# Expert layers: the key stage in whole slabs with a smaller search, the value stage on scaled weights with 16-bit low products

## The chip, the cores and the metric

One core of a Trainium2 chip runs the whole program. The metric is the device time in microseconds (us) from start to end of one execution; the median of several is compared.

## The reference

Two transformer layers on 256 tokens of width 2048, in f32: a state-space mixer, then sliding-window attention with a memory part, each followed by an output projection, a layer norm, an expert layer (PEER) and another layer norm. Only the expert layer matters here. For each token and each of 8 heads it scores 2 x 128 keys, takes the 16 best of each half, the 16 best of their 256 sums, and a softmax over those; the 128 chosen experts of 16384 then work as follows.

```python
sc = jnp.einsum('bshtd,htkd->bshtk', q, subkeys)
top_s, top_i = lax.top_k(sc, PEER_TOPK)
cand = top_s[..., 0, :, None] + top_s[..., 1, None, :]
best_s, best_c = lax.top_k(cand.reshape(b, s, PEER_HEADS, PEER_TOPK * PEER_TOPK), PEER_TOPK)
...
gate = jax.nn.softmax(best_s, axis=-1)
hid = jnp.einsum('td,tkd->tk', xb, u[ib])
act = jax.nn.gelu(hid, approximate=False) * gb
out = jnp.einsum('tk,tkd->td', act, v[ib])
x = layer_norm(DEEPNORM_ALPHA * x + out, g, b)
```

## The kernel before

Weights of 1 MiB slabs stream through the chip. SyncE loads a slab (2048 f32 columns in each of 128 partitions, two pieces) into one of three buffers `raw`. ScalarE copies each piece into `wh` (function `hi`, line 597), rounded to the fast matmul format fp32r; VectorE subtracts that from the original and so has the low rest (`lo`, lines 1743 and 1746). TensorE multiplies by the high and the low part (helper `mm`, line 1043), so that the sum is nearly f32. `wh` and the low buffers have four pieces. A semaphore `piece_used` counts pieces that TensorE is done with, `hi_ready` and `lo_ready` those made; a raw buffer is loaded anew when VectorE has lowered all of it.

The expert layer handles 64 of the tokens by rows and 192 densely:
- The 64 tokens: GpSimd gathers for each of 64 pairs of experts two rows to 128 partitions (1 MiB, two buffers). VectorE takes the product of a gathered key row with the token (a dot, L1928) and later adds the gathered value row, weighted, to an accumulator (L2126).
- The 192 tokens: key stage, 128 slabs of 128 experts each: h = gelu(U x) for all experts; then every h is multiplied by a gate, zero where the expert isn't chosen; value stage, 128 slabs: sum of V h.

Key stage, per slab (`slab_u`): for each of two pieces 8 products with `wh` over 384 columns (x's high and low part), then 8 with the 16-bit low part over 192. The low weights are scaled up by 2^16 so that 16 bits hold them (`scaled_up`). A fold (`cross` by ScalarE, L637, then one product) adds the side column group, and ScalarE applies gelu (L777). The first 64 slabs' h stay in SBUF (`KEPT`), the others' go to HBM and back.

During the first 64 key slabs VectorE makes the search, in 16 units of one head and 128 tokens: maxima, their places, removal, sums, maxima again; what it does beside the search is written out by hand in `UNIT_FILL`, L for a low of one piece, D for a dot. Some 18 dots stand there and 46 in the last 64 slabs (`DOT_PIECE`). Chosen places become expert numbers by one-hot comparison with `iota` and a sum, per unit. TensorE replicates the numbers (`replicate`) before slab 20 (`REP_TRIP`), and GpSimd can gather from then on. In the last 64 key slabs the gates are spread out: 48 groups of four tokens, each a comparison on VectorE (`compare`, L2051), scaled copies on ScalarE (`gate_rows`, L792) and 8 products on TensorE (`spread`).

Value stage, per slab (`slab_v`): for each of 2 pieces and 2 halves of 512 columns, five products: the first 64 of the 192 tokens (here "split": their high and low part side by side as one operand of 128 columns) with the high and the low weights, the other 128 ("whole") high by high, high by low, low by high. 20 products of 512 columns, all fp32r, on unscaled weights. ScalarE makes the activations' high part (L856) and its double (L857), VectorE the low part (L1760), and the gated h for the later slabs (L2105). The last two slabs have their own order (`last_slabs_v`), and a layer norm follows.

## Time and profile before

| | us |
|---|---|
| median of three executions | 3279.53 (3274.16 to 3283.69) |
| the profiled execution, its own time | 3274.78 |
| its span, first to last instruction | 3273.0 |
| TensorE / VectorE / ScalarE / GpSimd busy | 3196.3 / 2773.5 / 1997.0 / 406.6 |
| moved by DMA | 969.07 MB, mean 296 GB/s |
| TensorE's granted clock, mean | 0.996 of full |

Times in the trace are microseconds from the span's start, durations of groups are means in nanoseconds. An engine's busy time is the union of its instructions' times; matmuls are pipelined, so one's duration is longer than the distance to the next one's start. "L1043" is line 1043 of the kernel.

### The profile page before, as it was taken

What the parts mean: (1) busy time and instruction counts of PE and PEld (TensorE: products, weight loads), DVE (VectorE), ACT (ScalarE), POOL (GpSimd) and SP (SyncE); (2) the same over time, 40 slices, a digit from 0 to 9 for tenths busy, and PEclk for the clock granted to TensorE, in tenths of its full rate; (3) what the DMA queues carried; (4) which work ended last, traced back from release to release, by engine and by line L of the source; (5) the groups of instructions that cost most, each with busy time, mean ns of one, the idle gap of its engine ahead of it and who ended that gap; (6) DMA issues with size and microseconds to landing.
All of it is one profiled execution on the core that took longest, in us unless ns stands there. A gap on an engine that the chain in (4) does not pass through costs nothing. (4 is left out here: it accounts for less than half of the span.)

```text
span 3273.0 us, 52190 instructions
## 1 busy us (share of the span) xinstructions
PE 3196.3 (98%) x19468; PEld 2762.0 (84%) x19468; DVE 2773.5 (85%) x4026; ACT 1997.0 (61%) x3631; POOL 406.6 (12%) x266
## 2 busy tenths in 40 slices
PE   9999999999999999999999999999999999999998
PEld 8888888889888888888888887888888888888887
DVE  5775669999999888888887756999999988888887
ACT  4444556556898755555555545655688875555555
POOL 0000000011111122222100000001111112222220
PEclk9999999999999999999999999999999999999999
DMA  7553345698999989999984344578899999999995
GB/s 273 183 183 140 116 161 192 257 342 339 379 379 378 373 335 372 362 371 367 365 305 156 117 152 158 197 278 338 335 390 380 373 369 366 368 370 368 363 368 224
DMA packets 169221, 969.07 MB, mean 296 GB/s; under 512 B 18912, under 2 KB 52704, under 8 KB 55648
## 3 DMA queue, kind: packets, MB, share of 16 engines
q1 hardware_dynamic: 132192, 698.61, 56.2%
q0 software_dynamic: 36864, 268.45, 22.3%
q8 instruction: 80, 1.31, 0.1%
q14 instruction: 85, 0.70, 0.1%
HBM read 951.26 MB, written 15.73 MB: 295 GB/s over the span
## 5 line engine op out<-in xcount | busy, mean ns | idle before, releaser
L597 ACT ACTIVATE wh<-raw 128x1024 fp32r<-128x1024 f32 x1264 | 1335.5, 1060 | 833.5 <-PE ps L1043 663.9
L1043 PE MATMUL ps<-xx,wh 128*128 128x384 f32 (+1 forms) x5504 | 1333.7, 358 | 6.8 <-DVE xx L1755 4.0
L1043 PE MATMUL ps<-wh,act 128*128 128x512 f32 x3584 | 1190.6, 390 | 0.4 <-issue 0.2
L1746 DVE TENSOR_TENSOR wl<-raw,wh 128x1024 fp32r<-128x1024 f32 x752 | 905.9, 1221 | 323.8 <-ACT wh L597 322.2
L1043 PEld LDWEIGHTS ps<-xx,wh 128*128 128x128 f32 x5504 | 955.5, 189 | 73.5 <-issue 5.7
L1043 PE MATMUL ps<-wl,act 128*128 128x512 f32 x2304 | 897.6, 390 | 0.0
L1043 PEld LDWEIGHTS ps<-wh,act 128*128 128x128 f32 x3584 | 673.8, 188 | 142.0 <-DVE wl L1746 1.0
L1743 DVE SCALAR_TENSOR_TENSOR halves<-raw,wh 128x1024 f16<-128x1024 f32 x512 | 615.2, 1213 | 63.5 <-ACT wh L597 63.1
L1043 PEld LDWEIGHTS ps<-wl,act 128*128 128x128 f32 x2304 | 433.2, 188 | 89.7
L1043 PE MATMUL ps<-halves 128*128 128x192 f16 x4096 | 428.3, 248 | 22.5 <-DVE halves L1743 20.6
L1043 PEld LDWEIGHTS ps<-halves 128*128 128x128 f16 x4096 | 312.7, 98 | 112.4 <-issue 62.8
L1043 PE MATMUL ps<-xx,wl 128*128 128x256 f32 x1408 | 393.9, 280 | 0.0
L1711 POOL DMA_INDIRECT arena<-in_urows,idx x128 | 150.9, 1179 | 1907.3 <-DVE idx L2018 1072.0
L1711 POOL DMA_INDIRECT arena<-in_v,idx x128 | 246.8, 1928 | 839.4 <-DVE arena L2126 818.4
L2126 DVE SCALAR_TENSOR_TENSOR arena<-arena,hid 128x2048 f32<-128x2048 f32 x128 | 300.2, 2345 | 2.2 <-DMA arena<-in_v,idx 2.1
L1928 DVE SCALAR_TENSOR_TENSOR arena<-arena 128x2048 f32<-128x2048 f32 x128 | 292.0, 2281 | 0.0
L1043 PEld LDWEIGHTS ps<-xx,wl 128*128 128x128 f32 x1408 | 266.2, 189 | 0.5
L792 ACT ACTIVATE hot_w<-hot,x_space 128x128 f16<-128x128 f16 x768 | 242.1, 410 | 8.0 <-DVE hot L2051 8.0
L637 ACT ACTIVATE cross<-ps 128x192 fp32r<-128x192 f32 (+1 forms) x272 | 89.8, 330 | 124.5 <-PE ps L1043 122.2
L1043 PE MATMUL ps<-cross,ident_r 128*128 128x192 f32 (+1 forms) x272 | 92.0, 338 | 16.9 <-ACT cross L637 15.7
L777 ACT ACTIVATE arena<-ps 128x192 f32<-128x192 f32 x128 | 42.1, 329 | 108.3 <-PE ps L1043 108.2
L1043 PE MATMUL ps<-arena 64*128 64x128 f32 (+9 forms) x712 | 93.3, 317 | 7.5 <-DVE arena L2004 4.6
(225 smaller groups left out, 1751.2 us busy)
## 6 DMA issues: line engine op xcount, KB each, us to landing
raw<-in_u SPq DMA_DIRECT2D x256, 1024.0 KB, 7.1
raw<-in_v SPq DMA_DIRECT2D x256, 1024.0 KB, 7.4
raw<-in_w SPq DMA_DIRECT2D x118, 1024.0 KB, 4.8
h_scratch<-hring SPq DMA_DIRECT2D x128, 96.0 KB, 7.3
hring<-h_scratch SPq DMA_DIRECT2D x128, 96.0 KB, 7.1
arena<-in_memT SPq DMA_DIRECT2D x4, 512.0 KB, 7.2
raw<-in_w SPq DMA_DIRECT2D x4, 512.0 KB, 7.8
arena<-in_xT SPq DMA_DIRECT2D x4, 512.0 KB, 8.5
```

Source lines behind the costliest of these rows:

```text
L597: nc.scalar.activation(wh[:, j, :], raw_piece(p), ACT.Copy, scale=W_UP if scaled_up(p) else 1.0)\
L637: nc.scalar.activation(cross[:, 0:n], ps[:, bank, n:2 * n], ACT.Copy).then_inc(cross_out, 1)
L777: nc.scalar.activation(h_kept[:, k, :] if kept else hring[:, j, :], ps[:, j, 0:ND], ACT.Gelu, scale=W_DOWN).then_inc(evac_done, 1)
L792: nc.scalar.activation(hot_w[:, q % 2, w, t, :], one_hot(q, 0, t), ACT.Copy, scale=gate_hl[w][:, of // NS, of % NS:of % NS + 1]).then_inc( ...
L1043: return nc.tensor.matmul(out, lhs, rhs, start=start, stop=stop, **kw)
L1711: pool.indirect_dma_start(out=gbuf[n % SLOTS], out_offset=None, in_=rows_of, in_offset=bass.IndirectOffsetOnAxis(ap=idx[:, j:j + 1], axis=0))\
L1743: v.scalar_tensor_tensor(out=wl16[:, j, :], in0=raw_piece(p), scalar=W_UP, in1=wh[:, j, :].bitcast(F32), op0=ALU.mult, op1=ALU.subtract).t ...
L1746: v.tensor_tensor(wl[:, j, :], raw_piece(p), wh[:, j, :].bitcast(F32), ALU.subtract).then_inc(lo_ready, 1)
L1928: v.scalar_tensor_tensor(out=rows_u, in0=rows_u, scalar=1.0, in1=xrep, op0=ALU.mult, op1=ALU.mult, accum_out=hid[:, j:j + 1]).then_inc(slo ...
L2126: v.scalar_tensor_tensor(out=vacc, in0=rows_v, scalar=hid[:, j:j + 1], in1=vacc, op0=ALU.mult, op1=ALU.add).then_inc(slot_free, 1)
```

## The change

What it does:
- Key stage: high copies and lows are made for a whole slab by one instruction (`hi_slab`, `low_slab`), TensorE multiplies all 16 high parts, then all 16 low ones; the fold stands after the tenth high product. `piece_used` now counts the high and the low part of a slab.
- Search: two units at a time, interleaved; 112 candidate sums instead of 256 (4 x 16 and 12 x 4); the copy of the scores is gone; the one-hot selection is made for four units together in 16-bit numbers (`batch`). 24 dots in the first 64 slabs, 40 in the last. Replication before slab 16, the gates' transposition and setup at slabs 48 and 51 instead of 64 and after.
- Gates: one comparison for both halves of a group.
- Value stage: its weights are scaled by 2^16 too; what is added to its sums (the residual through `ident_up`, the accumulator, the gathered rows' weights, the norm's epsilon) is scaled likewise. The low products are 16-bit: four over 512 columns for the whole tokens and, for the split ones, only high weights' rest by a 16-bit copy of the activation (`a16`, a fourth copy on ScalarE), 64 columns wide, two products side by side on the two halves of the array. The 12 high products stay.

The diff, cut to its core:

```diff
-REP_TRIP = 5
+REP_TRIP, SEL_TRIP = 4, 12
...
-UNIT_FILL = ([("L", "", "L", "", "L", "L", "")] * 2 + [("L", "L", "L", "", "L", "L", "")]
-             + [("L", "L", "L", "L", "L", "L", "")] * 7 + [("LL", "LL", "LL", "LL", "LDL", "LL", "DL")]
-             + [("LDLL", "", "LDLL", "L", "LDLL", "L", "L")] * 4 + [("LDLL", "", "LLL", "L", "LDLL", "L", "L")])
-UNIT_TAIL = ("L", "LD", "L", "L", "L", "", "")
-SPARED = (2, 5)
...
+PAIR_FILL = ([("L", "", "L", "", "L", "", "L", "")] * 2 + [("L", "L", "L", "L", "", "", "", "")]
+             + [("S", "S", "", "S", "S", "", "S", "S"), ("S",) * 8,
+                ("S", "S", "", "S", "SD", "S", "D", "S"), ("S", "S", "SD", "S", "S", "SD", "S", ""),
+                ("S", "SD", "", "S", "S", "D", "S", "S")])
+LAST_FILL = ("S", "D", "S", "", "SD", "", "S", "", "S")
+REST_FILL = ("S", "SD", "SD", "SD", "S", "SD", "SD", "S", "SD", "SD") * 2
+BATCH = 4
+KEY_PAIRS = 4 * TOPK + (TOPK - 4) * 4
+EXP_SLAB, SETUP_SLAB = 40, 51
+DOT_SLABS = (1, 2, 4, 6, 7)
...
-    return P_U0 <= p < P_V0 or P_U1 <= p < P_V1
+    return P_U0 <= p < P_INB or P_U1 <= p < P_END
...
+        def hi_slab(p):
+
+            act.wait_ge(piece_used, p - (RING - 1))
+            act.wait_ge(lo_ready, p - 2)
+            n, j = p // 2, p % RING
+            act.wait_ge(raw_full[n % RAW_SLABS], 16 * (n // RAW_SLABS + 1))
+            nc.scalar.activation(wh[:, j:j + 2, :], raw[:, n % RAW_SLABS, :].rearrange("p (e c) -> p e c", e=2), ACT.Copy,
+                                 scale=W_UP if scaled_up(p) else 1.0).then_inc(hi_ready, 2)
...
+            def v_slab(k):
+                p, s = v0 + 2 * k, k % 2
+                act.wait_ge(piece_used, p - (RING - 1))
+                if k < KEPT:
+                    source = h_kept[:, k, :]
+                else:
+                    act.wait_ge(act_ready, layer * (S_EXP - KEPT) + k - KEPT + 1)
+                    source = act_t[:, s, :]
+                nc.scalar.activation(ffn_h[:, s, :], source, ACT.Copy).then_inc(acth_ready, 1)
+                nc.scalar.activation(ffn_dup[:, s, :], source[:, 0:NS], ACT.Copy).then_inc(dup_ready, 1)
+                if k:
+                    hi_slab(p)
+                act.wait_ge(piece_used, max(p - 2, v0))
+                nc.scalar.activation(a16[:, s, :], source, ACT.Copy).then_inc(a16_ready, 1)
...
+            pe.wait_ge(hi_ready, piece + 2)
+            for kc in range(KC):
+                last = mm(both, part(wh, kc), xx[:, kc, :, NS:], kc == 0, False, skip_group_check=True)
+                if kc == FOLD_AT and side_of is not None:
                     fold(side_of, 1 - par_, side_t0)
-                if then is not None:
-                    then(e)
+            last.then_inc(piece_used, 1)
+            if then is not None:
+                then(0)
+            pe.wait_ge(lo_ready, piece + 2)
+            for kc in range(KC):
+                if x_from is not None and kc % XS == 0:
+                    pe.wait_ge(x16_ready, x_from + kc // XS + 1)
+                last = mm(side, part(wl16, kc), x16[:, kc // XS, kc % XS, :], False, kc == KC - 1, skip_group_check=True)
+            last.then_inc(piece_used, 1)
...
+        def v_high(s, e, q):
+            w_hi = wh[:, 2 * s + e, q * 512:(q + 1) * 512]
+            return w_hi, ps[:, 2 * e + q, :], ps[:, 4 + 2 * e + q, :]
+
+        def split_low(s, e):
+
+            w = wl16[:, 2 * s + e, :]
+            mm(ps[0:NS, 2 * e, :], a16[:, s, 0:NS], w[:, 0:512], False, False, skip_group_check=True)
+            return mm(ps[NS:P, 2 * e + 1, :], a16[:, s, 0:NS], w[:, 512:PC], False, False, skip_group_check=True)
+
+        def whole_low(s, e, q):
+            return mm(ps[:, 4 + 2 * e + q, :], a16[:, s, NS:ND], wl16[:, 2 * s + e, q * 512:(q + 1) * 512], False, False,
+                      skip_group_check=True)
 
         def slab_v(piece, chunk, dup, s, opens=False):
 
             pe.wait_ge(actl_ready, chunk + 1)
             pe.wait_ge(dup_ready, dup)
             both, a_h, a_l = act[:, s, 0:2 * NS], ffn_h[:, s, NS:ND], ffn_l[:, s, NS:ND]
-            for e in range(2):
-                j = 2 * s + e
-                pe.wait_ge(lo_ready, piece + (e + 1))
-                for q in range(2):
-                    w_hi, w_lo = (w[:, j, q * 512:(q + 1) * 512] for w in (wh, wl))
-                    split, whole = ps[:, 2 * e + q, :], ps[:, 4 + 2 * e + q, :]
-                    mm(split, both, w_hi, opens, False, skip_group_check=True)
-                    mm(split, both, w_lo, False, False, skip_group_check=True)
-                    mm(whole, a_h, w_hi, False, False, skip_group_check=True)
-                    mm(whole, a_h, w_lo, False, False, skip_group_check=True)
-                    last = mm(whole, a_l, w_hi, False, False, skip_group_check=True)
-                last.then_inc(piece_used, 1)
-
...
+            def low_slab():
...
+                v.scalar_tensor_tensor(out=wl16[:, j:j + 2, :],
+                                       in0=raw[:, p // 2 % RAW_SLABS, :].rearrange("p (e c) -> p e c", e=2), scalar=W_UP,
+                                       in1=wh[:, j:j + 2, :].bitcast(F32), op0=ALU.mult, op1=ALU.subtract)\
+                    .then_inc(lo_ready, 2)
...
+                    own.mark(v.tensor_tensor(sums[:, 0:4 * TOPK].rearrange("p (a b) -> p a b", a=4),
+                                             tv[:, 0, 0:4].unsqueeze(2).broadcast_to([P, 4, TOPK]),
+                                             tv[:, 1, :].unsqueeze(1).broadcast_to([P, 4, TOPK]), ALU.add))
+                    own.mark(v.tensor_tensor(sums[:, 4 * TOPK:].rearrange("p (a b) -> p a b", b=4),
+                                             tv[:, 0, 4:TOPK].unsqueeze(2).broadcast_to([P, TOPK - 4, 4]),
+                                             tv[:, 1, 0:4].unsqueeze(1).broadcast_to([P, TOPK - 4, 4]), ALU.add))
...
+                elif step == 6:
+                    own.mark(v.tensor_tensor(pick.rearrange("p w k a u -> p (w k) a u"),
+                                             rank.rearrange("p w k u -> p (w k) u").unsqueeze(2)
+                                             .broadcast_to([P, 2 * TOPK, TOPK, BATCH]),
+                                             iota_u.unsqueeze(1).broadcast_to([P, 2 * TOPK, TOPK, BATCH]), ALU.is_equal))
+                elif step == 7:
+                    flat = pick.rearrange("p w k a u -> p w k (a u)")
+                    own.mark(v.tensor_tensor(flat, flat, top_f[:, b % 2].rearrange("p w a u -> p w (a u)").unsqueeze(2)
+                                             .broadcast_to([P, 2, TOPK, TOPK * BATCH]), ALU.mult))
+                else:
+                    for w in range(2):
+                        own.mark(v.tensor_reduce(
+                            sel[:, w, b * BATCH * TOPK:(b + 1) * BATCH * TOPK].rearrange("p (u k) -> p k u", u=BATCH),
+                            pick[:, w].rearrange("p k a u -> p k u a"), AX.X, ALU.add))
...
-                quad = slice(4 * q, 4 * q + 4)
-                for w in range(2):
-                    v.tensor_tensor(hot[:, q % 2, w, :].rearrange("p (a j t) -> p a j t", a=4, t=4),
-                                    iota_h.rearrange("p a (j t) -> p a j t", t=4),
-                                    sel_t[:, w, quad].unsqueeze(1).unsqueeze(1).broadcast_to([P, 4, P // 4, 4]),
-                                    ALU.is_equal).then_inc(onehot_ready, 1)
+                v.tensor_tensor(hot[:, q % 2, :, :].rearrange("p w (j t) -> p w j t", t=4),
+                                iota_h.rearrange("p (j t) -> p j t", t=4).unsqueeze(1).broadcast_to([P, 2, P, 4]),
+                                sel_t[:, :, 4 * q:4 * q + 4].unsqueeze(2).broadcast_to([P, 2, P, 4]),
+                                ALU.is_equal).then_inc(onehot_ready, 2)
...
+            def gated(k):
+
+                n = layer * (S_EXP - KEPT) + k - KEPT
+                dve.wait_ge(h_loaded[k % BODY], 16 * (n // BODY + 1))
+                dve.wait_ge(actl_ready, c0 + k - 1)
+                dve.wait_ge(a16_ready, layer * S_EXP + k - 1)
+                v.tensor_tensor(act_t[:, k % 2, :], hring[:, k % BODY, :], gate_of[:, k - KEPT, :],
+                                ALU.mult).then_inc(act_ready, 1)
```

## Rows read from the trace of the kernel before

**Rows 1.** Page, part 1: busy us, share of the span, instructions, each engine

```profile
PE 3196.3 (98%) x19468; PEld 2762.0 (84%) x19468; DVE 2773.5 (85%) x4026; ACT 1997.0 (61%) x3631; POOL 406.6 (12%) x266
```

**Rows 2.** Windows, layer 0: length, busy us of each engine, clock, DMA share, GB/s

```profile
520.32:814.14 293.82, 281.63 (x2156) 257.77 (x2155) 282.49 (x629) 167.89 (x262) 31.93 (x20) 0.99 0.79 295
814.14:1132.84 318.70, 307.43 (x2495) 279.36 (x2493) 295.94 (x362) 281.98 (x687) 48.04 (x47) 1.00 0.97 379
1133.94:1712.86 578.92, 578.81 (x2569) 479.37 (x2570) 497.82 (x515) 321.30 (x510) 122.54 (x62) 0.99 0.93 353
603.00:613.00 10.00, 7.69 (x48) 6.62 (x46) 9.96 (x30) 3.09 (x5) 0.00 (x0) 0.83 0.63 209
1000.00:1050.00 50.00, 48.40 (x397) 44.19 (x396) 46.46 (x58) 44.56 (x109) 7.31 (x7) 1.00 1.00 393
1200.00:1250.00 50.00, 50.00 (x223) 41.38 (x222) 44.12 (x41) 27.77 (x44) 15.66 (x7) 1.00 0.96 374
1550.00:1600.00 50.00, 50.00 (x222) 41.39 (x221) 43.21 (x50) 27.91 (x45) 9.41 (x5) 1.00 0.95 361
```

**Rows 3.** Timeline, TensorE in the key stage: start us, us, what

```profile
556.09 1.64 PE L1043 MATMUL ps<-xx,wh 128*128 128x384 f32 x8
557.57 0.83 PE L1043 MATMUL ps<-halves 128*128 128x192 f16 x8
...
558.36 1.58 PE L1043 MATMUL ps<-xx,wh 128*128 128x384 f32 x8
559.78 0.83 PE L1043 MATMUL ps<-halves 128*128 128x192 f16 x8
560.39 0.42 PE L1043 MATMUL ps<-xx,wh 128*128 128x384 f32 x1
```

**Rows 4.** Timeline, TensorE at half-wide products

```profile
530.10 0.83 PE L1043 MATMUL ps<-halves 128*128 128x192 f16 x8
530.87 3.71 PE L1043 MATMUL ps<-ident_r,arena 128*64 128x128 f32 x64
534.51 0.44 PE L1043 MATMUL ps<-xx,wh 128*128 128x384 f32 x1
```

**Rows 5.** Timeline, TensorE where the expert indices are replicated

```profile
605.88 0.83 PE L1043 MATMUL ps<-halves 128*128 128x192 f16 x8
609.00 0.49 PE L1043 MATMUL ps<-arena 128*128 128x128 f32 x2 [2.29 <-DVE arena L2004]
```

**Rows 6.** Timeline, VectorE: one search unit, and a dot with comparisons

```profile
539.03 0.29 DVE L1949 COPY arena<-arena 128x256 f32<-128x256 f32 x1
...
553.07 0.29 DVE L1949 COPY arena<-arena 128x256 f32<-128x256 f32 x1
...
1000.20 1.21 DVE L1743 SCALAR_TENSOR_TENSOR halves<-raw,wh 128x1024 f16<-128x1024 f32 x1
1001.34 2.28 DVE L1928 SCALAR_TENSOR_TENSOR arena<-arena 128x2048 f32<-128x2048 f32 x1
...
1003.55 0.80 DVE L2051 TENSOR_TENSOR hot<-x_space,sel_t 128x512 f16<-128x512 f16 x2
```

**Rows 7.** Groups, VectorE, 530 to 620 us: xcount, busy us, mean ns

```profile
L1989 DVE FIND_INDEX8 arena<-arena 128x8 uint32<-128x128 f32 x14 | 3.8, 284 | 0.0
...
L1951 DVE FIND_INDEX8 arena<-arena 128x8 uint32<-128x256 f32 x6 | 2.5, 419 | 0.0
```

**Rows 8.** Timeline, TensorE beside a gate group

```profile
898.21 0.64 PE L1043 MATMUL ps<-hot_w,hot 128*128 128x128 f16 x8
898.66 0.59 PE L1043 MATMUL ps<-xx,wh 128*128 128x384 f32 x2
```

**Rows 9.** DMA issues, second key half and value stage: KB, median us to landing

```profile
raw<-in_u SPq DMA_DIRECT2D x52, 1024.0 KB, 8.2
...
raw<-in_v SPq DMA_DIRECT2D x108, 1024.0 KB, 7.4
```

**Rows 10.** Groups, ScalarE, value stage: a copy of 2048 elements

```profile
L870 ACT ACTIVATE arena<-arena 64x2048 f32<-64x2048 f32 x1 | 1.9, 1919 | 0.0
```

467 lines of the change are left out of this document (242 added, 225 removed).

## The prediction

> **What bounds the kernel now.** I read the page first, then the windows by stage. TensorE is busy 98% of the span of 3273.0 us [rows 1]. But a busy share of a pipelined engine hides short stalls, so the second view matters more: the expert layer has three stages [rows 2], the key stage's first 64 slabs (294 us), its last 64 with the gate work beside them (319 us) and the 128 value slabs (579 us). Layer 1 repeats them. Together they are some 2380 of 3273 us; outside them only details of two layer norms change.
>
> The reader is to see that each stage has another neighbour at its limit. In the first, VectorE is busy 282.5 of 293.8 us. In the second, the DMA engines are busy 97% of the time. In the value stage TensorE never idles (578.8 of 578.9), with DMA at 93% on average; so only there is a TensorE instruction saved worth its full time, until the next limit.
>
> TensorE's own floor comes from the timeline [rows 3]: eight high products take 1.42 to 1.48 us, eight 16-bit ones 0.62, a fold 0.17; a key slab without any wait takes 560.39 - 556.09 = 4.30 us. A value slab is 20 products in 578.9 / 128 = 4.52 us [rows 2], 0.226 each.
>
> **Key stage, TensorE.** The whole-slab order goes high to low and back once instead of twice. The first group after a low one takes 1.48 instead of 1.42 [rows 3], so 0.06 is saved: floor 4.24 us, 64 x 0.06 = 4 us per half, if the other engines follow. The fold now comes some 0.5 us earlier in the slab and wants ScalarE's copy earlier.
>
> **Key stage, first half (-8 us a layer).** 63 slab intervals at 4.30 and the 64 small products in 534.51 - 530.87 = 3.64 us [rows 4] are 275 us; measured is 294, so 19 us are lost. What loses them:
> - The wait for the expert indices. TensorE stands before the product at 609.00 [rows 5]; it starts 609.00 - 605.88 = 3.12 us after the start of a group that takes 0.62, so 2.5 us, and after that idle stretch the granted clock falls to the lower level (1.2 GHz) for a while: 0.83 on the mean over those 10 us [rows 2], some 1.7 us more. After the change the indices come about slab 13, by the order written out, and are wanted at slab 16. I take -4.5.
> - VectorE. A search unit with six lows takes 553.07 - 539.03 = 14.04 us [rows 6]; less 6 x 1.14 (a low from its start to the next one's start, 1001.34 - 1000.20) that is 7.2 us. Sixteen units: 115 us. New unit: the copy of the scores goes; the 256 candidates become 112; the one-hot selection goes to batches of four units. Durations [rows 7] overlap by some 0.08 us; 128 more elements cost 0.135 us. That gives 3.8 us a unit, 61 us. A batch: two 16-bit operations of 2048 elements, which I price at the rate of the 16-bit comparison (two of 512 elements in 0.80 us [rows 6]: 0.36 each, start to start, 1.2 for 2048; at the f32 rate 2.2), two reductions of 1024 (1.1 each), and seven small ones: 5.8 us, up to 8. Four: 23 to 32. The search falls from 115 to 84 (93).
> - Lows as slabs: one of 2048 takes what the dot takes, 2.21 us start to start, against 2 x 1.14: 0.07 x 62 = 4 us less. Six dots more (24 for 18): +13 us.
>
> Sum on VectorE: -31 + 13 - 4 = -22 us of 294, so it no longer bounds the whole half. Locally it does: in the third pair of units four steps of a batch stand between lows, and slab 2 is then lowered some 2.6 us late; pairs 6 and 7 with their dots ask for about 33 us in the time of seven slabs (30), some 4 us. And 14 dots stand in the last 20 slabs: 1.7 MiB = 1.78 MB a slab, at 385 GB/s 4.63 us instead of 4.24, +7 us over those 20, where 3 are lost today. Sum: -4.5 (indices) - 4 (floor) - 10 (waits between slabs 10 and 44 now) + 2.6 + 4 + (7 - 3) = -8. Bounds: -19 (all waits gone) and +2.
>
> **Key stage, second half (-14 a layer).** Floor 64 x 4.24 + 48 x 0.45 (a gate group, 898.66 - 898.21, [rows 8]) = 293 us. Bytes: 64 slabs, 40 rows instead of 46, and 64 stores of 0.098 MB: 115 MB. The rate to divide by is what a full window shows: share 1.00 at 393 [rows 2]; I take 382 to 390, so 296 to 302, with a little loss 303 us against 318.7: I keep -14, since layer 1 repeats to within 1% only. What TensorE waits for ScalarE stays about as it is: that copies a slab in one instruction (2048 elements in 1.92 us, [rows 10]), but has to be done sooner. Bounds 0 and -24.
>
> **Value stage (-17 a layer).** TensorE: 12 high products of 0.226 = 2.71. The low ones now are 16-bit: 4 of 512 columns at, by [rows 3] (0.62/8 for 192), 0.21 = 0.86, and four half-wide ones in two pairs. That two half-wide products run side by side the trace shows: their 64 records fill 3.64 us [rows 4], 0.057 each, while two records of a full-width product of the same columns and type take 0.49 us with the pipeline's end in it [rows 5], 0.11 each by what is left. So a pair costs one: 0.43 for the four. Changing to half width and back costs something: the last full-width product starts about 530.10 + 7 x 0.083 = 530.68, the half-wide ones at 530.87, 0.19 for 0.083; I take 0.1 each way, 0.2 a slab. Sum 4.20 us, 0.32 less than today, 41 us over 128 slabs. (The Trainium skill, "TensorEngine Tiling (Array Packing)", Key Properties, says that changing the tiling mode drains the engine; it gives no time.)
>
> But DMA takes over. While h is kept in SBUF a slab brings 1.049 MB and 37/62 of a gathered row: 1.674 MB; later 1.049 + 27/56 rows + 0.098 of h = 1.652 MB. At 4.52 us that is 370 and 365 GB/s, and [rows 2] show 374 at a share of 0.96 and 361 at 0.95. Taken to a share of 0.985 that is some 382 and 374, and the slab can't be shorter than 4.38 and 4.42. 118 slabs at 4.40, ten without gathers at 4.20: 561 us, against 579 and, in layer 1, a little less: -17 on the mean. VectorE then needs 2.2 + 0.27 + 0.6 x 2.26 + small = 3.85 of 4.40, ScalarE gets a fourth copy but stands at 321 of 579 us [rows 2]. Bounds: -41, where DMA gives way, and 0.
>
> The Trainium skill puts the HBM limit of one core at about 358 GB/s ("DMA: Bandwidth & Descriptors", Where 436 GB/s comes from) and a core streaming alone at about 425 ("HBM Reference", Specifications). By the first the value stage could gain nothing: 1.674 MB / 358 = 4.68 us, more than today, but [rows 2] already stand above it, so the trace disagrees and it gets no chance. By the second DMA would need 3.94 us and TensorE would bound at 4.20, rival A below; no window of this trace reaches it over 50 us.
>
> Layer norms, the scaling of the accumulator (one ScalarE copy beside idle time), the moved gate setup: nothing, each hidden beside TensorE work; if uncovered, some 2 us each.
>
> **Sum.** 2 x (-8 - 14 - 17) = -78 us. The profiled execution took 3274.78; the median of three is 3279.53, 0.1% above. On the median's footing: about 3201. Changes under 0.3% (10 us) can't be told from none.
>
> **Rivals.**
> - A: TensorE bounds the value stage (DMA reaches over 400 GB/s): 2 x (-41 - 20 - 10) = -142: 3138. For: the value stage's share of 0.96 at 374 is not yet 1.00. Against: where it is 1.00 the rate was 393, and 4.20 us a slab want 399. Chance 0.17.
> - B: the value stage keeps its pace, because DMA is full as it is: only the key stage gains, 2 x -22: 3235. For: at 0.96 the share that is left is small, and a transfer that is late once is not made up. Against: the second key half runs at a share of 0.97 over 319 us [rows 2]. Chance 0.20.
> - C, the slower one: the ring of three raw slabs. A raw slab is free again only when one copy and one low of the whole slab are done, about 1.9 + 2.2 = 4.1 us after landing, while now the last piece is done 3.3 after it. The loop must close in 3 slabs: today 3 x 4.52 = 13.6 us. Landing 7.4 [rows 9] + 4.1 + up to 2.3 behind an accumulation is 13.8; with the 8.2 of the key stage 14.6, 4.87 us a slab: 118 x 0.33 = +39 a layer, less 22 in the key stage: 3279.5 + 34 = 3313. It decides where landing and queueing exceed 9.5 us. Against: the prefetch absorbs single late ones. Chance 0.06.
> - D: the gains are eaten: VectorE falls behind in the search (batches at the f32 rate and more) and DMA holds the value stage: 3280 +- 10. Chance 0.05.
> - My forecast: 0.52, by itself 3172 to 3230.
>
> Range: B with its edge above, A just below: 3135 to 3245 leaves out C, D and half of A, 0.19. Faster by over 0.3%: forecast, A and most of B, 0.87; same 0.06; slower 0.07.
>
> **What would show it.** Value slab interval 4.35 to 4.45 us, DMA share at or above 0.98 there, and ScalarE's copies waiting for DMA instead of for TensorE. First half of the key stage near 286 us, with no clock drop about slab 20; second near 303. Half-wide products starting in pairs, with 0.1 us lost before and after. The sum is wrong if the value slab comes out at 4.2 (A) or stays at 4.5 (B), if landing rises beyond 9 us (C), or if TensorE waits long for 16-bit lows in the first twenty key slabs (D).

## The result, and the profile after

Three more executions and the profiled one of the changed kernel have a median of 3234.29 us (3227.44 to 3248.78); the kernel before, run beside them, 3280.01. The medians differ by 46 us; the ratio, here and below formed from the means, is 0.9868, 95% interval 0.9831 to 0.9905: 1.3% less. Forecast was 3201, with a range of 3135 to 3245: the time lies in the range, near its upper end, but just outside the 3172 to 3230 that was given to the forecast's own mechanism. The profiled execution took 3227.44 us (3274.78 before), its span is 3225.6 (3273.0 before): of the -78 us of the sum it shows -47, so the sum was 31 too large.

The engines over the whole span, against [rows 1]:

```profile
PE 3147.4 (98%) x19468; PEld 2512.1 (78%) x19468; DVE 2667.2 (83%) x3291; ACT 1985.3 (62%) x3383; POOL 567.8 (18%) x266
```

The windows by stage of layer 0, against [rows 2] (same columns); the value stage stands as its first and second half. The fifth line is the stretch in which the indices are replicated now, the sixth the start of the experts in layer 1:

```profile
521.47:811.01 289.54, 277.44 (x2144) 264.72 (x2142) 255.50 (x445) 155.90 (x200) 45.64 (x26) 0.99 0.83 316
811.01:1117.19 306.18, 299.62 (x2497) 285.36 (x2496) 277.12 (x242) 276.21 (x623) 66.27 (x42) 1.00 0.98 379
1118.29:1402.95 284.66, 275.30 (x1281) 166.25 (x1282) 234.53 (x161) 162.99 (x253) 93.95 (x35) 1.00 0.92 357
1407.58:1683.85 276.27, 275.85 (x1260) 165.38 (x1259) 245.81 (x222) 164.48 (x253) 76.54 (x27) 1.00 0.94 367
...
586.00:596.00 10.00, 10.00 (x77) 9.66 (x76) 8.72 (x32) 5.96 (x7) 1.09 (x1) 1.00 0.68 228
...
2040.00:2080.00 40.00, 36.88 (x301) 35.08 (x299) 32.05 (x105) 19.37 (x27) 0.00 (x0) 0.91 0.56 205
```

By stage, both layers, after less before, beside the forecast for a layer:

| us | layer 0 | layer 1 | forecast |
|---|---|---|---|
| key stage, first 64 slabs | -4.3 | +0.6 | -8 |
| key stage, last 64 slabs | -12.5 | -15.4 | -14 |
| value stage | -13.4 | -11.8 | -17 |
| between key and value stage | 0.0 | +0.9 | 0 |
| outside (start, between the layers, end) | +8.4 in all | | 0 |

VectorE went from 282.5 to 255.5 busy us in the first stage (-27; forecast -22), and the first stage still gained next to nothing. The value stage's second half has TensorE busy without a stall; its first half moves fewer bytes a second and stalls.

TensorE in the second half of the value stage (timeline: start, us, instruction, count):

```profile
1509.66 0.38 PE L1069 MATMUL ps<-halves 128*64 128x512 f16 x2
1509.98 3.02 PE L1069 MATMUL ps<-wh,act 128*128 128x512 f32 x12
1512.84 1.59 PE L1069 MATMUL ps<-halves 128*128 128x512 f16 x8
1514.36 3.02 PE L1069 MATMUL ps<-wh,act 128*128 128x512 f32 x12
1517.22 1.59 PE L1069 MATMUL ps<-halves 128*128 128x512 f16 x8
```

High products 1512.84 - 1509.98 = 2.86 us, low ones 1514.36 - 1512.84 = 1.52: a slab takes 4.38, again and again. The forecast counted 2.71 + 1.49 = 4.20 for TensorE and 4.38 to 4.42 for DMA. The interval came out as forecast (4.35 to 4.45), but here TensorE sets it.

TensorE in the first key half, against [rows 3] to [rows 5]; the bracket is idle time and what ended it:

```profile
523.91 1.26 PE L1069 MATMUL ps<-xx,wh 128*128 128x384 f32 x6
528.29 1.49 PE L1069 MATMUL ps<-halves 128*128 128x192 f16 x16 [3.12 <-DVE halves L1967]
...
589.25 0.41 PE L1069 MATMUL ps<-arena 128*128 128x128 f32 x2
...
591.36 1.26 PE L1069 MATMUL ps<-xx,wh 128*128 128x384 f32 x6
592.46 1.49 PE L1069 MATMUL ps<-halves 128*128 128x192 f16 x16
593.73 1.99 PE L1069 MATMUL ps<-xx,wh 128*128 128x384 f32 x10
595.56 0.25 PE L1069 MATMUL ps<-cross,ident_r 128*128 128x192 f32 x1
595.65 0.54 PE L1069 MATMUL ps<-xx,wh 128*128 128x384 f32 x2
...
751.72 1.52 PE L1069 MATMUL ps<-halves 128*128 128x192 f16 x11 [2.37 <-DVE halves L1967]
```

Three things are to be seen. The wait for the indices and the clock drop behind it are gone (589.25 has no bracket; clock 1.00 from 586 to 596, 0.83 in [rows 2]). Slab 2 waits 3.12 us for its low part (forecast 2.6). A key slab is 1.10 + 1.27 + 1.83 + 0.09 = 4.29 us, not 4.24: against 4.30 in [rows 3] the whole-slab order is worth 0.01, not 0.06.

VectorE just before the last of these waits:

```profile
740.59 2.28 DVE L1967 SCALAR_TENSOR_TENSOR halves<-raw,wh 128x2048 f16<-128x2048 f32 x1
746.17 2.29 DVE L1985 SCALAR_TENSOR_TENSOR arena<-arena 128x2048 f32<-128x2048 f32 x1 [3.30 <-DMA arena<-in_urows,idx]
...
749.38 2.28 DVE L1967 SCALAR_TENSOR_TENSOR halves<-raw,wh 128x2048 f16<-128x2048 f32 x1
```

It stood 3.30 us before rows that had not landed, with the low part that TensorE wanted behind them in its order.

### The profile page after: what moved, and what is told of

It reads as the page before. It is cut to its first block, busy times and chain, and to the rows that moved or that the text cites. A ratio compares the mean times of both kernels' runs of the same rounds, so it can differ in the third digit from the quotient of the medians.

```text
span 3225.6 us, 51808 instructions
## 1 busy us (share of the span) xinstructions
PE 3147.4 (98%) x19468; PEld 2512.1 (78%) x19468; DVE 2667.2 (83%) x3291; ACT 1985.3 (62%) x3383; POOL 567.8 (18%) x266
## 4 chain that ended last, share of the span: by engine, by line
PE 41%; DMA 15%; DVE 9%; ACT 6%; issue 3%; ACTq 0%; SPq 0%; DVEq 0%
PE ps L1069 41%; DMA raw<-in_v 6%; DVE halves L1967 4%; DMA arena<-in_v,idx 3%; ACT wh L629 3%; DMA raw<-in_u 3%; ACT hot_w L821 2%; DMA h_scratch<-hring 2%; DVE arena L2211 1%; DMA arena<-in_urows,idx 1%; DMA raw<-in_w 1%; DVE arena L1985 1%; DVE xx L1802 0%; DVE wl L1793 0%; ACT hring L806 0%
## 5 line engine op out<-in xcount | busy, mean ns | idle before, releaser
L1967 DVE SCALAR_TENSOR_TENSOR halves<-raw,wh 128x2048 f16<-128x2048 f32 x508 | 1161.2, 2287 | 209.8 <-issue 124.0
L629 ACT ACTIVATE wh<-raw 128x2048 fp32r<-128x2048 f32 x508 | 970.1, 1910 | 196.6 <-DMA raw<-in_v 149.4
L1069 PE MATMUL ps<-wh,act 128*128 128x512 f32 x3584 | 936.6, 400 | 14.6 <-ACT wh L629 14.5
L1069 PE MATMUL ps<-halves 128*128 128x192 f16 (+2 forms) x6144 | 795.8, 294 | 26.6 <-DVE halves L1967 26.2
L1069 PEld LDWEIGHTS ps<-halves 128*128 128x128 f16 (+1 forms) x6144 | 447.0, 100 | 301.2 <-issue 206.7
L1758 POOL DMA_INDIRECT arena<-in_urows,idx x128 | 215.7, 1685 | 1811.4 <-DVE idx L2103 1015.7
L1758 POOL DMA_INDIRECT arena<-in_v,idx x128 | 343.3, 2682 | 723.6 <-DVE arena L2211 700.1
L1793 DVE TENSOR_TENSOR wl<-raw,wh 128x1024 fp32r<-128x1024 f32 x240 | 292.4, 1221 | 158.7 <-ACT wh L615 157.8
L615 ACT ACTIVATE wh<-raw 128x1024 fp32r<-128x1024 f32 x248 | 259.4, 1057 | 265.0 <-PE ps L1069 232.6
L1985 DVE SCALAR_TENSOR_TENSOR arena<-arena 128x2048 f32<-128x2048 f32 x128 | 292.3, 2283 | 38.3 <-DMA arena<-in_urows,idx 38.2
L1069 PE MATMUL ps<-wl,act 128*128 128x512 f32 x256 | 99.6, 389 | 0.0
```

The costliest lines, as they stand in the source:

```text
L615: nc.scalar.activation(wh[:, j, :], raw_piece(p), ACT.Copy, scale=W_UP if scaled_up(p) else 1.0)\
L629: nc.scalar.activation(wh[:, j:j + 2, :], raw[:, n % RAW_SLABS, :].rearrange("p (e c) -> p e c", e=2), ACT.Copy, scale=W_UP if scaled_up(p ...
L1069: return nc.tensor.matmul(out, lhs, rhs, start=start, stop=stop, **kw)
L1758: pool.indirect_dma_start(out=gbuf[n % SLOTS], out_offset=None, in_=rows_of, in_offset=bass.IndirectOffsetOnAxis(ap=idx[:, j:j + 1], axis=0))\
L1793: v.tensor_tensor(wl[:, j, :], raw_piece(p), wh[:, j, :].bitcast(F32), ALU.subtract).then_inc(lo_ready, 1)
L1967: v.scalar_tensor_tensor(out=wl16[:, j:j + 2, :], in0=raw[:, p // 2 % RAW_SLABS, :].rearrange("p (e c) -> p e c", e=2), scalar=W_UP, in1=w ...
```

## The experiments

Each kernel is the changed one with one edit unless said. Ratios are to the kernel before, which ran on the same chip. All stage lengths below come from the profiled executions, one for each kernel. The key halves are marked by the starts of ScalarE's gelu of slabs 0, 63 and 127; "kept" is from the first to the 65th copy of a value factor, "second" from there to the last.

| us, layer 0 / 1 | first key | second key | kept | second |
|---|---|---|---|---|
| before | 293.8 / 294.1 | 318.7 / 315.0 | 294.5 / 291.8 | 284.4 / 284.4 |
| after | 289.5 / 294.8 | 306.2 / 299.6 | 289.3 / 287.9 | 276.3 / 276.5 |
| alternating | 293.6 / 293.5 | 306.9 / 301.8 | 306.5 / 298.6 | 265.8 / 265.3 |
| full width | 291.6 / 291.7 | 306.2 / 301.2 | 291.9 / 287.6 | 282.9 / 282.7 |
| no rows | 283.4 / 281.3 | 296.1 / 296.1 | 278.4 / 278.4 | 275.9 / 275.9 |
| fill | 291.1 / 292.2 | 298.7 / 299.6 | 286.7 / 293.0 | 280.1 / 281.5 |
| low first | 292.9 / 293.5 | 309.6 / 301.2 | 285.5 / 292.1 | 275.8 / 278.2 |
| rows 31/33 | 300.8 / 291.6 | 302.8 / 301.3 | 278.4 / 280.0 | 284.8 / 276.1 |
| all | 292.0 / 291.3 | 304.6 / 300.1 | 266.3 / 266.3 | 290.0 / 292.3 |
| one by one | 294.5 / 296.4 | 305.0 / 300.0 | 307.6 / 306.1 | 304.1 / 304.1 |
| all, rows 34/30 | 287.6 / 288.3 | 303.8 / 298.7 | 277.8 / 275.8 | 286.9 / 289.8 |
| third buffer | 291.7 / 294.9 | 304.8 / 301.5 | 285.8 / 287.4 | 275.7 / 280.9 |
| all, third buffer | 289.5 / 285.0 | 300.3 / 303.0 | 284.2 / 284.0 | 263.5 / 264.1 |
| placed | 290.3 / 290.2 | 303.6 / 301.8 | 281.8 / 276.2 | 269.1 / 268.6 |

The second key half has the same code in all of them but the first, and with its gathers takes 298.7 to 309.6 us: where transfers press, a stage's length in one execution is good to some 5 us either way. (The fill kernel has the changed kernel's value stage unaltered, and its kept half took 286.7 and 293.0 us, its second 280.1 and 281.5.) Without rows the two layers agree to 0.2 us there.

**Full width, and one by one: what the half-wide pairs cost**

```diff
-            mm(ps[0:NS, 2 * e, :], a16[:, s, 0:NS], w[:, 0:512], False, False, skip_group_check=True)
-            return mm(ps[NS:P, 2 * e + 1, :], a16[:, s, 0:NS], w[:, 512:PC], False, False, skip_group_check=True)
+            mm(ps[:, 2 * e, :], a16[:, s, 0:P], w[:, 0:512], False, False, skip_group_check=True)
+            return mm(ps[:, 2 * e + 1, :], a16[:, s, 0:P], w[:, 512:PC], False, False, skip_group_check=True)
```

> The changed kernel, but the split tokens' four low products of a value slab are full-width again (128 columns of the factor, one after the other, still in 16 bits) in place of two side-by-side pairs. This takes the change to the half-wide form away and adds 0.2 us of products. It adds products of whole tokens into the lower rows of the split tokens' banks, so the output is another. Theory 1 (a pair costs 0.236 and the two changes of width 0.09 each, as in the changed kernel's trace): low part 8 x 0.2165 + 0.09 = 1.82 against 1.52 + ..., counted from the starts: 4.38 - (0.236 + 2 x 0.309) + 4 x 0.2165 - 0.09 = 4.39 + 0.01, so 4.39 to 4.46 us a slab without a wait: side by side is worth at most 0.08 us a slab, 10 us a layer where TensorE bounds, and the time is 3235 to 3250. Theory 2 (the pairs give the 0.43 us that two full-width products take, as the change means them to): 4.38 + 0.43 = 4.81 a slab, over 4.52 of the kernel before: 3285 us or more.

3250.23 us, ratio 0.9899 (0.9875 to 0.9923); the output is another. The second edit leaves the columns at 64 and writes both to `ps[0:NS, ...]`.

> The changed kernel, but the four half-wide low products of the split tokens run one after the other, all in the upper 64 columns of the array, instead of two and two side by side. The output is the reference's. If two half-wide products really run at the same time and one takes 0.215 us on its own, the value slab without a wait goes from 4.38 to 4.81 us: half-wide products alone would be worse than full-width ones (4.48 to 4.49 in the full-width run). If the pairs had run one behind the other in truth, it stays at 4.38. The second half of the value stage: 303 us against 276; the whole time some 95 us more, 3325 to 3335.

3328.18 us, one execution. Timelines of the full-width kernel, then of the one-by-one kernel:

```profile
1510.86 1.90 PE L1069 MATMUL ps<-halves 128*128 128x512 f16 x8
1512.41 3.09 PE L1069 MATMUL ps<-wh,act 128*128 128x512 f32 x12
1515.35 1.90 PE L1069 MATMUL ps<-halves 128*128 128x512 f16 x8
```

```profile
1510.84 3.04 PE L1069 MATMUL ps<-wh,act 128*128 128x512 f32 x12
1513.72 2.02 PE L1069 MATMUL ps<-halves 128*128 128x512 f16 x8
1515.67 3.04 PE L1069 MATMUL ps<-wh,act 128*128 128x512 f32 x12
```

A slab takes 1515.35 - 1510.86 = 4.49 us with full-width products and 1515.67 - 1510.84 = 4.83 one by one, 4.38 in pairs. (0.227 and 0.216 below are the distances of starts inside these groups.) So a pair does run side by side: two pairs save 4.83 - 4.38 = 0.45, the 0.43 of the forecast. And the full-width slab is 12 x 0.227 + 8 x 0.216 = 4.45 and 0.04: going from f32 to 16 bits and back costs almost nothing. Two products less, 0.43, made only 4.49 - 4.38 = 0.11: the way to half width and back costs 0.32 a slab, where I had taken 0.2. The starts of single products in the changed kernel say where it goes: 0.309 in place of 0.216 us before the first half-wide pair, 0.309 again behind the last one, 0.240 for the first pair, and 0.338 in place of 0.227 for the high product behind them: 0.09 + 0.09 + 0.02 + 0.11.

**Alternating order: one change of width for two slabs, and who bounds then** (`flipped` is true for odd slabs)

```diff
+            if flipped:
+                for e in range(2):
+                    split_low(s, e)
+                for e in range(2):
+                    for q in range(2):
+                        last = whole_low(s, e, q)
...
+                if flipped:
...
+                    for h in range(2):
+                        act.wait_ge(raw_full[p // 2 % RAW_SLABS], 16 * (p // 2 // RAW_SLABS + 1))
+                        nc.scalar.activation(wh[:, p % RING + h, :], raw_piece(p + h), ACT.Copy, scale=W_UP)\
+                            .then_inc(hi_ready, 1)
...
+                if k > 1 and s:
+                    low_half(k, 0)
+                    low_half(k, 1)
```

For the odd slabs ScalarE copies two pieces ahead of the value factors, and VectorE makes their two low parts first of all; an even slab's low part still stands behind the row that is due.

> The changed kernel, but every odd value slab takes its products in the reverse order: first the two side-by-side pairs and the four whole low ones in 16 bits, then the twelve high ones. So a run of low products goes through two slabs, and for two slabs there is one change from high to 16 bits, one to the half-wide form, one back, one to the high form, in place of two each. The output is the reference's. Theory 1 (the changes between forms cost the 0.31 us that the last starts of a group showed in the changed kernel's trace, about 0.31 + 0.04 a slab): two slabs without a wait take 8.76 - 0.31 to 0.35 = 8.41 to 8.45 us instead of 8.76, 4.21 to 4.23 a slab. Theory 2 (the longer starts belong to the products wherever they stand): 4.38 a slab stays, no gain. What the time does under theory 1 depends on who bounds the stage: if TensorE alone does, the 128 slabs fall from 565 to about 543 us, -22 a layer, 3190 us in all. If the transfers do (0.95 to 0.98 of their engines' time in the second half of the stage already, and the copies in the first half waiting for them), the stage falls by 5 to 10 us a layer, to 555 to 560, the share goes to 0.98 in both halves, and the time is 3215 to 3225.

3233.06 us, ratio 0.9833 (0.9807 to 0.986). Windows of its kept and of its second half:

```profile
1240.00:1300.00 60.00, 54.06 (x251) 34.02 (x252) 47.34 (x38) 32.72 (x57) 17.59 (x7) 0.97 0.89 343
...
1500.00:1600.00 100.00, 99.77 (x478) 64.73 (x477) 92.75 (x96) 62.01 (x108) 32.91 (x12) 1.00 0.98 391
```

The changes of width are the cost: the second half falls from 276 to 265 us, 4.21 a slab. (Where no row stands before an even slab's low part it is 8.31 for two slabs, 4.16 each.) There DMA delivers 391 GB/s beside a TensorE that is busy 99.77 of 100 us. So DMA does not bound that half at 4.38, which the forecast had it do. The kept half, with 0.60 gathered row a slab in place of 0.48, gets slower by 11 to 17 us at 343 GB/s, so that the whole gains nothing that can be measured against the changed kernel. Part of that is the clock: it was 0.97 in the window above, where the changed kernel had 1.00.

**No rows: what the transfers cost where**

```diff
-            pool.indirect_dma_start(out=gbuf[n % SLOTS], ...)
+            if n % (2 * PAIRS) < SLOTS:
+                pool.indirect_dma_start(out=gbuf[n % SLOTS], ...)
```

(The edit also lets VectorE's dots multiply by nought and fits its waits; the output is another.)

> The changed kernel without the gathers of rows after the first two of each layer: VectorE does every dot product and every addition of rows, on rows that stand still in the two buffers (multiplied by nought in the dots), so its work and TensorE's stay and about a third of the bytes of the expert layer goes. It tells what the transfers cost in each stage. Theory 1 (after the change the transfers hold the second key half and the first half of the value stage, and VectorE the first key half): first key half 289.5 us falls by the 3.5 to 4.5 us that TensorE loses among its last 20 slabs, to 285, the rest of its loss stays with VectorE; second key half 306.2 and 299.6 fall to 280 to 290 (64 slabs at 4.30 and 32 groups of gate products in the gaps, which the kernel before has too); kept half of the value stage 284.7 falls to 281 (64 x 4.38); second half stays at 276. Sum 2 x (-4 - 18 - 4) = -52, 3180 us. Theory 2 (the loss of the value stage is in its own waits, ScalarE's order of copies and VectorE's additions, not in bytes): the kept half keeps 284 to 285.

3173.61 us, ratio 0.9656 (0.963 to 0.9683). All value slabs run at 4.38. The rows' transfers cost 10 us in the kept half and none in the second; 3.5 and 10 in the second key half; and 6.2 and 13.5 in the first, mostly between slabs 44 and 63 (19 intervals), that take 82.5 us here and 90.2 and 92.3 in the changed kernel. The wait before slab 2 (3.12 us) and, in layer 0, one of 2.2 in the seventh pair stay: those are VectorE's order.

**Fill: VectorE's order in the search**

```diff
-PAIR_FILL = ([...] * 2 + [("L", "L", "L", "L", "", "", "", "")]
-             + [("S", "S", "", "S", "S", "", "S", "S"), ("S",) * 8,
+PAIR_FILL = ([...] * 2 + [("L", "L", "L", "LS", "", "S", "", "")]
+             + [("S", "S", "", "S", "", "S", "", "S"), ("S", "", "SS", "S", "SS", "S", "", ""),
```

> The changed kernel with another order of VectorE's work in the gaps of the search: the low parts of slabs 2 and 3 are taken in the third pair instead of the fourth (the first of them some 5 us earlier), and the lows and dots of pairs four to eight are moved by one to three gaps, one dot of the seventh pair to the eighth; counts are the same (38 lows and 8 dots). The output is the reference's. Theory 1 (VectorE's order makes TensorE wait in the first key half: 3.1 us before slab 2, 2.2 + 0.5 + 0.9 + 0.3 us in the seventh and eighth pair, by the idle times before its low products in the changed kernel's trace): those 7.0 us of 11.6 go, the first key half takes 282 to 284 us in layer 0 instead of 289.5, and layer 1, where slab 2 waits longer, gains 7 to 10; the time is 3216 to 3222. Theory 2 (VectorE is short of time in this stage as a whole, whatever the order: 62 lows and 24 dots at 2.2 us and 84 us of search are 273 of some 280 us): the waits only move, the half stays within 2 us of 289, the time at 3230 to 3234.

3222.97 us, ratio 0.9804 (0.9779 to 0.983). Slabs 0 to 44 take 195.2 and 196.2 us against 199.4 and 202.5, without the wait before slab 2; in layer 1 that wait also brought the clock down (0.91 from 2040 to 2080, 1.00 in this run). But slabs 44 to 63 take 95.9 and 96.0 instead of 90.2 and 92.3. One of VectorE's waits there:

```profile
729.14 2.29 DVE L1985 SCALAR_TENSOR_TENSOR arena<-arena 128x2048 f32<-128x2048 f32 x1 [5.85 <-DMA arena<-in_urows,idx]
```

Both theories hold in their part: the order cost 4 to 6 us a layer in the first 44 slabs, and in this execution what it gave was taken back, 5.7 and 3.7 us of it, where 14 dots stand in 20 slabs. The median is lower than that suggests: its interval ends just below the changed kernel's 0.9831, and the profiled execution (3228.86) was one of the two slowest of six. Where the other executions gained is not on record.

**Why the kept half stalls: three edits**

Low part before the rows (`low_slab()` moved ahead of the loop of additions):

> The changed kernel, but in the value stage VectorE takes the low part of a slab before it adds the rows that are due in that slab, not after. Nothing else is moved. Without the gathers the kept half (the first 64 value slabs) took 278 us instead of 288 to 289, with every slab at 4.38; with them it moves 343 to 372 GB/s and stalls, while the alternating kernel moved 389 to 402 GB/s in the second half without a stall. So the engines of the transfers can do more than the kept half asks (383 GB/s at 4.38 us a slab). Theory 1 (coupling: VectorE stands before rows that have not landed, 16.7 us in the kept half of the changed kernel; the low behind them is late, its raw buffer comes free late, and the next slab's load starts late): the kept half falls by 3 to 8 us a layer, and the time by 6 to 15 us, to 3220 to 3228. Theory 2 (the transfers are short of bandwidth there, whatever the order): no change, 3230 to 3238. A third case: the rows' additions are now later, their two buffers come free later, and the waits for rows grow: slower by some 5 us.

3234.22 us, ratio 0.9849 (0.9823 to 0.9875): the kept half 285.5 and 292.1. No effect; the coupling through VectorE's order is not it.

A third buffer for the value rows:

> The changed kernel with a third buffer for the value rows from the thirteenth row of a layer on, in the place of the first eleven kept slabs' factors, which are used up by then. Nothing else is moved: 37 and 27 rows, low after rows. The bytes are the same. Theory 1 (the turn of the two buffers: in the kept half a row of the changed kernel is added 14.7 us after the one two before it, and 9.5 us lie between the end of its issue and its addition, with a shortest landing of 6.6): with three the turn is 22 us, the waits of VectorE for rows (16.8 us in the kept half) go, and the kept half falls from 285 to 289 to 278 to 281 us, the floor without gathers; the time to 3215 to 3225. Theory 2 (the sum of bytes, or how the rows and the slabs share the engines): the raw slabs are late as before or later, since the rows are now fetched earlier: no gain, 3230 to 3240.

3229.77 us, ratio 0.9849 (0.9826 to 0.9873): 285.8 and 287.4. Waits of the kept half (who waited for whom, us in total, times, longest), first in the changed kernel, then in this one:

```profile
ACT wh L629 <- DMA raw<-in_v: 73.7, 31, 4.6
...
DVE arena L2211 <- DMA arena<-in_v,idx: 16.7, 13, 2.7
```

```profile
ACT wh L635 <- DMA raw<-in_v: 58.5, 29, 4.7
...
DVE arena L2222 <- DMA arena<-in_v,idx: 2.0, 2, 1.3
```

VectorE's waits for rows are nearly gone, and the raw slabs still come late, about as often. My theory of the two buffers' turn falls.

Fewer rows in the kept half (`ACC_KEPT = 31`):

> The changed kernel, but 31 of the 64 rows are added in the kept half of the value stage and 33 in the second half, in place of 37 and 27: 0.50 and 0.59 a slab in place of 0.60 and 0.48. Theory 1 (the two buffers of rows and the waits for them limit the kept half; a buffer's turn is 14.6 us there against 18.3 us in the second half): the kept half falls from 288.6 to 280 to 283 us; the second half, now with a turn of 17 us, stays within 3 us of 276. The time falls by 8 to 14 us. Theory 2 (bandwidth): the kept half gains what the second loses, since the sum of bytes is the same; the time stays within 4 us of 3234.

3230.15 us, ratio 0.9844 (0.9812 to 0.9876): the kept half falls to 278.4 and 280.0, its floor; the second takes 284.8 and 276.1 with 33. So the number of rows a slab decides, and not how the rows are buffered. Of the three only this edit moved the half; as a whole it can't be told from the changed kernel.

**All together, and the place of a row**

Alternating order, fill, low first, 31 and 33 rows:

> All that the runs so far point to, in one kernel with the reference's output: value slabs in alternating order (4.21 us a slab in its second half, 265.5 us), VectorE's order of the search's gaps from the fill run, the low part before the rows, and 31 and 33 rows. Theory 1 (the kept half of the alternating kernel, 299 to 307 us, was slow by the coupling of rows, lows and raw buffers): the kept half falls to 270 to 280, the second half to 265 to 270, so the value stage to 545 from 565 us, and with 5 us a layer of the key stage the time is 3175 to 3195. Theory 2 (the alternating order itself wants the odd slab's copy and low part within one slab's time, and that does not fit with 0.5 row a slab at 4.21): the kept half stays at 290 or more, the time at 3205 to 3220.

3211.14 us, ratio 0.9775 (0.9753 to 0.9797). The kept half runs at 8.31 us for two slabs (266.3 in all), the second half takes 290 to 292, with VectorE waiting 0.6 us for rows. Then 34 and 30 rows:

> The kernel of the run with everything (alternating value slabs, VectorE's order of the search's gaps, low part before the rows), but 34 of the 64 rows in the kept half and 30 in the second, in place of 31 and 33. That run had no stall in its kept half (266.3 us, 4.20 a slab) and lost 24 to 26 us in the second (290 and 292), where VectorE was busy 258.8 of 290 us and never stood before rows (0.6 us). Theory 1 (at 4.21 us a slab the second half has no room on VectorE for 0.59 row a slab: low 2.2, act's low and gate product 0.6, row 1.3 = 4.1 in 4.21, and 0.54 gives 4.0; the first alternating run with 0.48 had none of it): the second half falls to 266 to 275; the kept half, with 0.55 a slab, stays at 266 to 275. The time falls from 3211 by 25 to 40 us, to 3170 to 3186. Theory 2 (a rate of rows in time decides in both halves: 0.48 in 4.21 us went without a stall, 0.60 in 4.38 stalled, and 0.55 in 4.21 is 0.131 a us against 0.137): both halves stall a little, 275 to 285 each, and the time is 3190 to 3210.

3218.1 us, ratio 0.9826 (0.9802 to 0.9849). Neither theory: the second half stays at 287 to 290 with fewer rows. Its timeline tells why. TensorE, at two places of one half:

```profile
1482.10 5.82 PE L1079 MATMUL ps<-wh,act 128*128 128x512 f32 x24
1487.76 1.59 PE L1079 MATMUL ps<-halves 128*128 128x512 f16 x8
1490.72 1.59 PE L1079 MATMUL ps<-halves 128*64 128x512 f16 x8 [1.36 <-DVE halves L1811]
1491.96 5.82 PE L1079 MATMUL ps<-wh,act 128*128 128x512 f32 x24
...
1521.82 5.82 PE L1079 MATMUL ps<-wh,act 128*128 128x512 f32 x24
1527.49 2.99 PE L1079 MATMUL ps<-halves 128*128 128x512 f16 x16
1530.13 5.82 PE L1079 MATMUL ps<-wh,act 128*128 128x512 f32 x24
```

VectorE at the same places (L1988 an even slab's low, L1811 an odd slab's, L2244 a row):

```profile
1483.84 2.29 DVE L1988 SCALAR_TENSOR_TENSOR halves<-raw,wh 128x2048 f16<-128x2048 f32 x1 [1.31 <-issue]
1486.05 2.35 DVE L2244 SCALAR_TENSOR_TENSOR arena<-arena,hid 128x2048 f32<-128x2048 f32 x1
1488.31 2.35 DVE L1811 SCALAR_TENSOR_TENSOR halves<-raw,wh 128x1024 f16<-128x1024 f32 x2
...
1523.78 2.29 DVE L1988 SCALAR_TENSOR_TENSOR halves<-raw,wh 128x2048 f16<-128x2048 f32 x1
1526.13 2.36 DVE L1811 SCALAR_TENSOR_TENSOR halves<-raw,wh 128x1024 f16<-128x1024 f32 x2
1528.41 0.35 DVE L1828 TENSOR_TENSOR act<-act_t,act 128x192 fp32r<-128x192 f32 x1
1528.68 0.35 DVE L2206 TENSOR_TENSOR act_t<-hring,arena 128x192 f32<-128x192 f32 x1
1528.95 2.35 DVE L2244 SCALAR_TENSOR_TENSOR arena<-arena,hid 128x2048 f32<-128x2048 f32 x1
```

In the first stretch the row stands between the even and the odd slab's low part, and two slabs take 1491.96 - 1482.10 = 9.86 us; in the second it stands behind the odd one, and they take 1530.13 - 1521.82 = 8.31. 28 rows in 56 slabs fall on odd slabs alone, 30 do not.

It was the "low first" edit, carried over, that put a row there. In the alternating kernel, without it, VectorE did the following in the second half:

```profile
1479.56 2.35 DVE L2242 SCALAR_TENSOR_TENSOR arena<-arena,hid 128x2048 f32<-128x2048 f32 x1
1481.83 2.28 DVE L1988 SCALAR_TENSOR_TENSOR halves<-raw,wh 128x2048 f16<-128x2048 f32 x1
1484.03 2.36 DVE L1811 SCALAR_TENSOR_TENSOR halves<-raw,wh 128x1024 f16<-128x1024 f32 x2
```

The row (L2242) of an even slab stands before that slab's low part, and two slabs took 8.45 us: 0.14 lost, not 1.55. An edit without effect in one order of products was a harmful one in the other.

With a third buffer, 36 and 28 rows:

> The kernel of the run with everything, with a third buffer for the value rows and 36 rows in the kept half, 28 in the second. If the turn of two buffers was the limit of the kept half, then it runs at 4.20 to 4.25 a slab with 0.58 row a slab, 266 to 272 us, the second half at 265 to 270, and the time is 3165 to 3180. If bytes are the limit (0.58 row a slab at 4.21 is 1.58 MiB = 1.66 MB in 4.21 us, 394 GB/s; 389 to 402 GB/s is the most that a stretch has shown), the kept half takes 275 to 290 and the time is 3185 to 3205.

3195.0 us, ratio 0.9755 (0.9731 to 0.978): the second half 264, the kept half 284, as under the second theory. Last, rows placed by hand, 35 and 29:

```diff
+                due = sum(1 for n in range(3, min(k, 121) + 1) if n % 2 or n in (30, 40, 50, 60))
```

> The kernel of the run with everything and a third buffer, but the rows of the value stage are placed by hand: one after the low part of every odd slab from 3 to 121 (60 rows), and four more after the even slabs 30, 40, 50 and 60 of the kept half; so 35 in the kept half, 29 in the second, where the run before had 36 and 28 by an even count. Reverse-order slabs are the odd ones, and their low part is wanted soonest. In the kernel with 34 and 30 rows, the pairs of slabs whose row fell after the even slab took 9.84 us, the others 8.31, in one and the same stretch. Theory 1 (the place of the row: behind the even slab's low it stands before the odd slab's, which TensorE then waits for): the second half takes 264 to 267 us with all its rows in odd slabs although it has one more; the kept half 266 + 4 x (1.5 to 3) = 272 to 278 us instead of 284; the time falls by 12 to 24 us from 3195, to 3170 to 3185. Theory 2 (bytes: 35 rows in the kept half are nearly the 36 of before): the kept half stays at 281 to 286, the time at 3190 to 3200.

3188.09 us, ratio 0.9706 (0.9688 to 0.9724), the fastest here: 3% below the kernel before. The second half carries one row more at 269 us (forecast 264 to 267; in layer 0 some 3.7 of the 5.6 us over the run before fall at one place near the end, where TensorE waits 2.39 us for a copy of a late raw slab and 0.80 for a low part), the kept half fell by 2 and 8 us (forecast 6 to 12), and the time is 3 us above its forecast. The place of a row is shown for the second half, by the pairs of slabs above; in the kept half it accounts for a part.

## Why the prediction was off, point by point

- **Key slab floor, -4 a half: not there.** 4.29 us against 4.30. The failed step is "the first group after a low one takes 1.48 instead of 1.42". The group of 1.42 in [rows 3] stands behind a low one too, with the fold between them, and that fold took 0.17 where a fold within high products, as now, takes 0.09 (595.56 to 595.65). So 1.42 was no group without a return, and the two did not show what a return costs.
- **Index wait, -4.5: right.** No idle before the product, clock 1.00.
- **VectorE's search, -31: right.** With the dots and lows -22 was forecast for the stage and -27 measured; 6 of the 16 units now run before the stage's first mark, 3 did before. A pair of units without a batch takes 7.6 us in the gaps between its lows, 3.8 each as priced.
- **Slab 2 late by 2.6: 3.12**, right, with 2.5 us more in layer 1, where the clock fell after it (10.03 us to the next gelu against 7.57).
- **Last 20 slabs, +7 - 3: too low.** Their 19 intervals took 90.2 and 92.3 us against 85.1 and 86.3: +5 to +6. The edit that gave VectorE time earlier made them 96. The slabs before them gained 9.4 and 5.4 us, where the terms of the sum make about 10.7. This term, the floor and layer 1's clock are why the first half gained 2 a layer on the mean, not 8.
- **Second key half, -14: right** (-12.5 and -15.4), at 379 and 384 GB/s where 382 to 390 were taken.
- **Value stage, -17: -13.4 and -11.8, and for another reason.** The failed step is the term "Changing to half width and back ... 0.2 a slab": it is 0.32, shown by the full-width and the one-by-one kernels. The 0.2 counted the gap before the half-wide products and one like it behind, but not that the first high product behind them takes 0.11 more. With 0.04 for going to 16 bits and back and some 0.02 of rounding TensorE's floor is so 4.38 instead of 4.20, and by luck it equals what I had taken for DMA. "But DMA takes over" is wrong for the second half (391 GB/s at 4.21 without a stall) and right for the kept half, which loses 10 us to the rows' transfers; but not at a share of 0.985: it runs at 0.92 to 0.94. The sign that was named fits this: ScalarE's copies wait 73.7 us for raw slabs in the kept half and 5.0 in the second. In time the second half came out as the terms of the forecast have it (276), and the kept half 8 to 9 us above its 64 x 4.38 = 280. One gain was in no term: in layer 0 the opening slab took 9.03 us before, with a clock of 0.93 from 1134 to 1180, and takes 6.28 now with 1.00.
- **Everything outside, 0: +8.4,** and 0.9 between the stages of layer 1. The last two value slabs cost 0.67 us each time (TensorE at 1688.69 waits for a low part) and the layer norm behind the value stage waits 3.44 us for ScalarE, 2.79 before; from the last copy of a value factor to the end of that wait it is 14.7 us, 12.2 before, in both layers. About 1 of these 2.5 us is no loss: the last copy now stands that much earlier ahead of TensorE's last products. Another 2.2 between the layers go with a granted clock of 0.91 from 1845 to 1885, where it was 1.00 before; what brought it down was not found. The stages begin 1.2 us later from the start.
- **Rivals.** The time is B's (3235), its mechanism is not: the value stage did not keep its pace. A's mechanism (TensorE bounds) is the second half's, at 4.38. C's mechanism, the ring of three raw slabs, is what the trace shows where the kept half stalls, see below, though not C's size: it cost 10 us a layer, not 39. So the time lies in the range with A's, B's and C's mechanisms each in part at work. The sum closes: 12 us short in the first key half, 9 in the value stage, 9 outside the stages, of 31.

**What stays open.** The kept half delivers 357 and 361 GB/s in the changed kernel (343 in a window of the alternating one, 376 in the last but one) with raw slabs late, at 0.60 row a slab, while the second half of the run with 33 rows carried 0.59 without a stall in one of its two layers. It is neither VectorE's waits for rows nor the turn of their buffers; of what was tried only fewer rows cure it. What the trace adds is the ring of the raw buffers. In the kept half of both layers (from 60 us in), where a copy had to wait, 14.3 us lay between it and the copy three slabs before, in the same buffer, and TensorE's pace wants 3 x 4.38 = 13.1: 1.9 for the copy, 1.2 until VectorE began the low part, 2.2 for it, 0.4 until SyncE had issued the load, and 8.6 from there to the next copy. The loads went out as soon as a buffer was free, and came too late. Why they take so long at 0.60 row a slab is not shown, and a fourth raw buffer, which would open the ring, was not tried.

## What to carry to other kernels

A form change is a price for the group, not for an instruction: before narrowing products to run them side by side, multiply what a change costs (0.32 us in and out here) by how often it happens, and order the groups so that two of them share it. When one engine serves several deadlines in order, move the work with the loosest one behind the tightest, and try the order anew when the deadlines change: the same row cost nothing, 0.14 or 1.55 us by its place. And where transfers are near full, time won ahead of a dense stretch can be given back in it: spread the transfers first.
